# A hybrid decoder layer on one core: the order of the end of the kernel, of GpSimd's scatter and gather, and of the expert-row layout

## The reference

```python
h = h + moe_ffn(rms_norm(h, norm_ffn_w[l]), router_w[l], ...)   # top 4 of 32
#   per block of tokens of one expert e:
#     gu  = xb @ w_gate_up[e] + b_gate_up[e]
#     act = glu * sigmoid(1.702 * glu) * (lin + 1)      (clamped)
#     y   = (act @ w_down[e] + b_down[e]) * gate
#   out[token] += y
h = rms_norm(h, norm_final_w)
return h[:, N_META:]
```

## Time and profile before

| what | value |
|---|---|
| median of 3 runs | 1507.97 us (1507.8 to 1509.02) |
| the profiled execution, its time | 1512.59 us |
| its span, first to last instruction | 1511.0 us |
| TensorE busy | 1486.2 us (98%) |
| VectorE, ScalarE, GpSimd busy | 618.4, 255.5, 331.2 us |
| mean granted TensorE clock | 0.998 of full |
| bytes moved by DMA | 484.29 MB, 321 GB/s over the span |

### The profile page before, as it was taken

One profiled execution on the slowest core, in us unless ns is written; L12 is line 12 of the kernel. 1 busy time (PEld: TensorE's weight loads), 2 busy tenths in 40 slices (PEclk: granted clock), 3 DMA queues, 4 the chain that ended last, 5 costly groups with the idle time before them and its releaser, 6 DMA issues.

```text
span 1511.0 us, 38177 instructions
## 1 busy us (share of the span) xinstructions
PE 1486.2 (98%) x15435; PEld 793.7 (53%) x15435; DVE 618.4 (41%) x1268; ACT 255.5 (17%) x348; POOL 331.2 (22%) x518
## 2 busy tenths in 40 slices
PE   8999999999999999999999999999999999999997
PEld 6998998977873333443344333343333433334443
DVE  6667989868445312321132211222112321113226
ACT  3533433356231000000000000000000000000002
POOL 2000000000023432332223322233222233222330
PEclk9999999999999999999999999999999999999999
DMA  3642232322338999999999999999999999999976
GB/s 135 248 162 86 112 112 111 148 102 81 154 129 294 412 417 418 419 416 418 419 419 417 413 414 410 416 415 409 413 406 414 411 414 410 412 416 413 411 313 278
DMA packets 81367, 484.29 MB, mean 321 GB/s; under 512 B 17518, under 2 KB 18162, under 8 KB 26418
## 3 DMA queue, kind: packets, MB, share of 16 engines
q1 hardware_dynamic: 66066, 459.14, 74.9%
q0 software_dynamic: 15264, 24.63, 4.4%
HBM read 467.54 MB, written 25.00 MB: 326 GB/s over the span
## 4 chain that ended last, share of the span: by engine, by line
PE 69%; DMA 19%; SPq 6%; DVE 4%; issue 1%; ACT 1%; POOL 0%; DVEq 0%; ACTq 0%; POOLq 0%
PE bank L1816 42%; DMA ring<-in_moe 17%; PE bank L1497 15%; SPq L490 6%; PE bank L1688 6%; DVE w_lo L962 1%; DMA ring<-in_w_in 1%; PE bank L1625 1%; PE bank L1628 1%; PE bank L1757 0%; PE bank L1640 0%; PE bank L1626 0%; PE bank L1655 0%; DVE reg_tq L1052 0%; DMA reg_vcs<-in_xT 0%
## 5 line engine op out<-in xcount | busy, mean ns | idle before, releaser
L1816 PE MATMUL bank<-ring,moe_f 128*32 128x512 f32 (+1 forms) x12216 | 995.9, 486 | 6.7 <-DMA ring<-in_moe 3.6
L1816 PEld LDWEIGHTS bank<-ring,moe_f 128*32 128x32 f32 x12216 | 388.7, 110 | 612.8 <-issue 370.2
L1405 DVE STREAM_TRANSPOSE moe_f<-bank 128x768 f32<-128x768 f32 x32 | 31.5, 983 | 629.6 <-PE bank L1816 622.5
L621 POOL DMA_INDIRECT moe_f<-n_scratch,idx_next x96 | 100.1, 1043 | 450.2 <-DVE moe_f L1387 426.6
L1497 PE MATMUL bank<-n_hi,w_hi 128*128 128x258 f32 (+2 forms) x608 | 190.6, 313 | 2.9 <-DVE w_lo L962 2.9
L1497 PE MATMUL bank<-n_lo,w_hi 128*128 128x258 f32 (+2 forms) x608 | 186.3, 306 | 0.0
L1497 PE MATMUL bank<-n_hi,w_lo 128*128 128x258 f32 (+2 forms) x608 | 186.3, 306 | 0.0
L906 ACT ACTIVATE moe_f<-moe_f 128x768 f32<-128x768 f32 x32 | 27.0, 844 | 735.2 <-DVE moe_f L1409 735.2
L1497 PEld LDWEIGHTS bank<-n_hi,w_hi 128*128 128x128 f32 x608 | 114.4, 188 | 10.9 <-issue 3.2
L1497 PEld LDWEIGHTS bank<-n_lo,w_hi 128*128 128x128 f32 x608 | 114.5, 188 | 6.8 <-issue 1.7
L1497 PEld LDWEIGHTS bank<-n_hi,w_lo 128*128 128x128 f32 x608 | 114.5, 188 | 5.5
(11 more groups left out here) (293 smaller groups left out, 1058.4 us busy)
## 6 DMA issues: line engine op xcount, KB each, us to landing
ring<-in_moe SPq DMA_DIRECT2D x381, 1024.0 KB, 26.6
ring<-in_w_in SPq DMA_DIRECT2D x24, 1024.0 KB, 5.9
expert_rows<-reg_k POOLq DMA_DIRECT2D x8, 1024.0 KB, 6.3
ring<-in_w_out SPq DMA_DIRECT2D x8, 1024.0 KB, 5.4
ring<-expert_rows SPq DMA_DIRECT2D x8, 1024.0 KB, 12.1
ring<-acs_scratch SPq DMA_DIRECT2D x4, 1024.0 KB, 6.7
idx_raw<-slot_table POOLq DMA_DIRECT2D x140, 0.8 KB
reg_vcs<-in_xT SPq DMA_DIRECT2D x4, 528.0 KB, 6.8
```

The lines of the kernel that those rows point to most:

```text
L621: g.indirect_dma_start(out=xg[:, n, :], out_offset=None, in_=n2_parts, in_offset=bass.IndirectOffsetOnAxis(ap=idx_next[:, 2 * n:2 * n + 1] ...
L1405: v.transpose(glu.rearrange("p b (g r) -> p g b r", g=GRANULES), gate).then_inc(gate_raw, 1)
L1816: ins = mm(out[l * LANE:(l + 1) * LANE, g * width:(g + 1) * width], x[:, at, g * LANE:(g + 1) * LANE], w[:, l * width:(l + 1) * width], st ...
```

## The change

Six edits. VectorE's activations of the last block go to a buffer of their own, `act_last`, without the wait for `dn_used`, outside the loop. In GpSimd's loop the scatter (with its wait) stands ahead of the gather and the list. The rows of `expert_rows` are ordered token by token (row t * 4 + k) where they are written (the value table) and where they are read. In the end VectorE adds the rows of tile m+1 before it scales the mean of tile m, and PE's part after that. The last tile is scaled and stored in two halves. The zeros of `reg_k` are written behind the constants. Four semaphores that nothing used are gone.

```diff
+        act_last = view(moe_f, 8448, FF_BLOCKS, BLOCK)
 # SP
-                rows = yk_d.rearrange("(k t) d -> t k d", k=TOPK)[m * P:(m + 1) * P]
+                rows = yk_d.rearrange("(t k) d -> t k d", k=TOPK)[m * P:(m + 1) * P]
-            for m in range(TT):
+            for m in range(TT - 1):
                 sp.wait_ge(o_ready, m + 1)
                 sp.dma_start(out_d[m * P:(m + 1) * P, :], o_sb[m]).then_inc(out_out, 16)
+            for hf in range(2):
+                c = slice(hf * 512, (hf + 1) * 512)
+                sp.wait_ge(o_ready, TT + hf)
+                sp.dma_start(out_d[(TT - 1) * P:, c], o_sb[TT - 1][:, c]).then_inc(out_out, 16)
 # GpSimd, start
-            steps.done(g.memset(reg_k[:, :], 0.0))
...
-            g.iota(v3[:, :, :, 1], pattern=[[P * LANES, TT], [SEQ * LANES, TOPK]], ...)
+            g.iota(v3[:, :, :, 1], pattern=[[P * TOPK * LANES, TT], [LANES, TOPK]], ...)
...
             pool.dma_start(table_d..., pad_tile).then_inc(table_filled, 16)
+            steps.done(g.memset(reg_k[:, :], 0.0))
+            steps.settled()
 # GpSimd, loop
+                hold((y_ready, j + 2))
+                scatter()
                 hold((xT_ready, j + 3))
                 gather()
                 base = pool.value_load(...)
                 list_rows(base)
-
-                hold((y_ready, j + 2))
-                scatter()
                 hold((idx_in, ...), (x_in, ...), (y_out, ...))
 # VectorE
-                dve.wait_ge(dn_used, j * DN + 2 * DN)
-                v.tensor_tensor(act_t, up, sig, ALU.mult).then_inc(act_ready, 1)
+                if not last:
+                    dve.wait_ge(dn_used, j * DN + 2 * DN)
+                v.tensor_tensor(act_last if last else act_t, up, sig, ALU.mult).then_inc(act_ready, 1)
...
-            with dve.Fori(2, n_blocks) as j:
+            with dve.Fori(2, ahead) as j:
                 activations(j, expert_of(j))
+            activations(ahead, last, last=True)
...
+            rows(0)
+            total(0)
             for m in range(TT):
+                if m + 1 < TT:
+                    rows(m + 1)
                 dve.wait_ge(h2_ss, TT + m + 1)
                 v.tensor_scalar(small[:, m:m + 1], ...).then_inc(o_ms, 1)
                 if m + 1 < TT:
-                    combine(m + 1)
+                    total(m + 1)
-                (root, reciprocal, scale of the whole tile)
+                scale(m)       # for the last tile in two halves of 512 columns
 # TensorE
-            down(n_blocks - 1, GU)
+            down(n_blocks - 1, GU, act_last)
```

More of the change, by code:

```diff
@@ L318, in build @@
         staged, conv_ready, xbc_ready = sem("staged"), sem("conv_ready"), sem("xbc_ready")
-        dt_done, dt_raw, dt_e = sem("dt_done"), sem("dt_raw"), sem("dt_e")
+        dt_done, dt_e = sem("dt_done"), sem("dt_e")
         acs_ready, wend_e, pk_ready, dtk_done, dtk_ready = (
@@ L339, in build @@
         first_kept, first_turned, stack_ready, xT_half = [sem("first_kept0"), sem("first_kept1")], sem("first_turned"), sem("stack_ready"), sem("xT_half")
-        n2T_done, n2T_ready, logit_done, top_ready, gate_e, m_ready = (
-            sem("n2T_done"), sem("n2T_ready"), sem("logit_done"), sem("top_ready"), sem("gate_e"), sem("m_ready"))
+        n2T_done, n2T_ready, logit_done, top_ready, gate_e = (
+            sem("n2T_done"), sem("n2T_ready"), sem("logit_done"), sem("top_ready"), sem("gate_e"))
         rank_done, pos_ready, table_out, list_ready, list_out, list_in = (
@@ L345, in build @@
             sem("idx_in"), sem("idx_moved"), sem("x_in"), sem("xT_ready"), sem("lane_ready"))
-        bias_in, up_raw, bias_ready = sem("bias_in"), sem("up_raw"), sem("bias_ready")
+        bias_in, bias_ready = sem("bias_in"), sem("bias_ready")
         gu_used, dn_used, gu_free, glu_ready, sig_ready, act_ready = (
@@ L524, in _ @@
             for m in range(TT):
-                rows = yk_d.rearrange("(k t) d -> t k d", k=TOPK)[m * P:(m + 1) * P]
+                rows = yk_d.rearrange("(t k) d -> t k d", k=TOPK)[m * P:(m + 1) * P]
                 for hf in range(2):
                     sp.dma_start(yk(m, hf), rows[:, 2 * hf:2 * hf + 2, :]).then_inc(yk_in[hf][m], 16)
-            for m in range(TT):
+            for m in range(TT - 1):
                 sp.wait_ge(o_ready, m + 1)
                 sp.dma_start(out_d[m * P:(m + 1) * P, :], o_sb[m]).then_inc(out_out, 16)
-            sp.wait_ge(out_out, 16 * TT)
+            for hf in range(2):
+                c = slice(hf * 512, (hf + 1) * 512)
+                sp.wait_ge(o_ready, TT + hf)
+                sp.dma_start(out_d[(TT - 1) * P:, c], o_sb[TT - 1][:, c]).then_inc(out_out, 16)
+            sp.wait_ge(out_out, 16 * (TT + 1))
         @block.gpsimd
@@ L562, in _ @@
             g.iota(v3[:, :, :, 0], pattern=[[P * LANES, TT], [0, TOPK]], base=0, channel_multiplier=LANES).then_inc(consts, 1)
-            g.iota(v3[:, :, :, 1], pattern=[[P * LANES, TT], [SEQ * LANES, TOPK]], base=0, channel_multiplier=LANES).then_inc(consts, 1)
+            g.iota(v3[:, :, :, 1], pattern=[[P * TOPK * LANES, TT], [LANES, TOPK]], base=0, channel_multiplier=TOPK * LANES).then_inc(consts, 1)
             b2 = blocks[:, 0:2 * EXPERTS].rearrange("p (e t) -> p e t", t=2)
@@ L1395, in _, with activations @@
             dve.wait_ge(bias_ready, 1)
-            def activations(j, e, follows=True, at=0):
+            def activations(j, e, follows=True, at=0, last=False):
                 def bias_col(k, b):
@@ L1436, in _ @@
             activations(1, 1, at=5)
-            with dve.Fori(2, n_blocks) as j:
+            ahead = dve.value_load(blocks[0:1, 2 * LIST + 5:2 * LIST + 6], min_val=EXPERTS - 1, max_val=LIST - 2)
+            with dve.Fori(2, ahead) as j:
                 activations(j, expert_of(j))
+            activations(ahead, last, last=True)
             roots[0] += 1
@@ L1460, in _, with rows @@
             ins.then_inc(diag_ready, 1)
-            def combine(m):
+            def rows(m):
                 dve.wait_ge(yk_in[1][m], 16)
@@ L1469, in combine, with total @@
                     acc = o_sb[m]
+            def total(m):
                 dve.wait_ge(part_done, m + 1)
@@ L1473, in combine, with scale @@
                                 ).then_inc(o_sum, 1)
-            combine(0)
+            def scale(m):
+                rooted()
+                steps.done(v.reciprocal(small[:, m:m + 1], small[:, m:m + 1]))
+                steps.settled()
+                for c in ([slice(0, D)] if m < TT - 1 else [slice(0, 512), slice(512, D)]):
+                    v.scalar_tensor_tensor(o_sb[m][:, c], o_sb[m][:, c], small[:, m:m + 1], w_fin[:, c], ALU.mult, ALU.mult
+                                           ).then_inc(o_ready, 1)
+            rows(0)
+            total(0)
             for m in range(TT):
+                if m + 1 < TT:
+                    rows(m + 1)
                 dve.wait_ge(h2_ss, TT + m + 1)
@@ L1479, in _ @@
                 if m + 1 < TT:
-                    combine(m + 1)
[L1481 to L1485, removed]
+                    total(m + 1)
+                scale(m)
         @block.tensor
@@ L1836, in gate_up, with down @@
                         between()
-            def down(j, moved=0):
+            def down(j, moved=0, x=act_t):
                 pe.wait_ge(act_ready, j + 2)
@@ L1849, in down @@
                         b = 2 * (q - GU) + u
-                        ins = lanes(3, QUARTER, act_t, b, slot(s)[:, u * D:(u + 1) * D], b == 0, b == FF_BLOCKS - 1)
+                        ins = lanes(3, QUARTER, x, b, slot(s)[:, u * D:(u + 1) * D], b == 0, b == FF_BLOCKS - 1)
                     ins.then_inc(dn_used, 1)
```

## The result

| | before | changed |
|---|---|---|
| median, first comparison (4 runs each) | 1508.49 us | 1518.23 us |
| ratio | | 1.0055, 95% interval 1.0044 to 1.0067 |
| profiled execution, span | 1511.0 us | 1519.2 us |
| mean granted TensorE clock | 0.998 | 0.994 |

The changed kernel is slower, by 8.3 us on the ratio; its interval runs from 6.6 to 10.1 us, and the two medians lie 9.7 us apart.

The account below looks back on a forecast made before the run. TensorE's work or DMA loads were taken to bound the blocks, then a chain of scatter, rows read back and TensorE's products; 6.1 + 0.2 - 0.4 = +5.9 us on 1507.97 gave 1513.9 us, range 1509.0 to 1517.0.

Parts of the forecast that it names:

- Release: At the end, TensorE's first product with the rows waits for last_of behind the last list: +6.1 us, ends 5.1 to 7.4.
- the cover: Steady blocks: the later gather still lands 9 us before VectorE wants the tokens, so it costs 0.
- The clock: First eight products after TensorE's longer idleness at the end run at a lower clock: +0.2 us, ends 0 and 2.2.
- Own buffer: TensorE's last down: the wait for VectorE's multiplication goes, TensorE gains 0.3 us there, worth 0 in the total.
- Rows first: VectorE's end: rows of tile 1 fill a 1.22 us wait, but TensorE's part bounds the sum: at most 0.1 us, taken as 0.
- Halves: Last tile's multiplication and store in two: -0.4 us net, ends +0.1 and -1.2.
- Zeros: Program's start: constants ready 1.8 us sooner, but a product then waits longer for ScalarE's squares: 0.
- Layout: Rows read back in one 8 KB run per partition: worth 0, as the loads have 6 us more to arrive.
- The fast landing: Rival at the end: the last list lands 2.6 us after issue, total +2.7 us, 1510.7; chance 0.08.
- No new wait: Rival at the end: the release of last_of never decides, only the halves count, 1507.5 us; chance 0.06.
- the weight loads gain: Rival in the 19 slow blocks: half of their 17.3 us to the DMA engines comes back, 1505.3 us; chance 0.09.
- my sign of being wrong: Product still waiting for expert_rows, list landing within 4 us, or the blocks' pace moving by more than 0.1 us.

Follow-up runs that it names:

- e1: Kernel before with only the order in GpSimd's loop changed, scatter ahead of gather and list: 1517.01 us against 1509.7, ratio 1.0047.
- e3: Changed kernel with GpSimd's last iteration cut to scatter, its landing and one move of indices, without last gather and list: 1507.19 us, 0.9982 of the kernel before.
- e5: Kernel before with the own buffer for the last activations alone: 1508.98 us against 1509.88, ratio 0.9995.
- e7: Kernel before with rows of tile m+1 ahead of the mean of tile m and the last tile in halves, alone: 1508.71 us against 1509.88, ratio 0.999.
- e12: Kernel before with scatter ahead of gather and list and the last iteration cut, no other edits: 1508.87 us against 1509.94, ratio 0.9991.
- e9: Kernel before with the zeros of reg_k behind the constants, alone, on another chip: 1533.14 us against 1532.83, ratio 1.0001.
- e6: Kernel before with expert_rows ordered token by token, alone: 1508.94 us against 1509.88, ratio 0.9992.
- e10: e3 plus two unused 128x512 products behind TensorE's last down, on the chip of e9: 1522.6 us, 0.9931 of the kernel before.
- e11: The changed kernel once more, on the chip of e9: 1530.58 us, 0.9988 of the kernel before.
- e4: Changed kernel with nine unused 128x512 products behind TensorE's last down: 1514.12 us, 1.0034 of the kernel before.

## Why the prediction was right

**The place and the sign** were right, on the chips of the first two groups and of the first comparison: list at the tail, `last_of` as the new release, the delay passed on in full, steady blocks unchanged. Measured and forecast side by side, from the profiles: list issued 9.37 us behind the eviction (forecast 9.4), landing 8.48 us (7.9, ends 6.85 and 8.43), first move to VectorE's copy 1.31 (1.30), copy to TensorE's start 1.37 (1.37). Release +6.63 us (+6.1), shown by e1 and, with the list left out, by e3. Two side readings were off without touching the sum. VectorE's idle time before the copy was 20.21 us, not some 16: the own buffer had let its last multiplication run earlier (e1, without that buffer, has 15.84). And the gather in a steady block starts 5.7 us behind the eviction where it had started 5.2 us ahead of it, so 10.9 us later and not "some 7"; the cover held all the same, as the pace shows.

**The clock** was mis-sized: I took +0.2 with an end of +2.2, it was +1.31. The sentence behind the 0.2, "the rows' clock was low for about 3.4 of those 4 us already", reads its window rightly. What failed is the conclusion that little was left to lose, which takes the clock to come back as soon behind the long gap as before. The kernel before in windows of 1 us:

```profile
1481.00:1482.00 1.00, 1.00 (x3) 0.29 (x2) 0.12 (x1) 1.00 (x1) 0.00 (x0) 0.63 0.98 406
...
1484.00:1485.00 1.00, 1.00 (x2) 0.28 (x2) 0.96 (x2) 0.00 (x0) 0.00 (x0) 0.66 1.01 414
1485.00:1486.00 1.00, 1.00 (x4) 0.48 (x3) 0.77 (x1) 0.00 (x0) 0.00 (x0) 1.00 1.05 426
```

There the clock was low from 0.6 to 4.0 us behind the start of the eight products. In the changed kernel it was low from their start to 6.1 us behind it. That is 2.7 us more at half the clock, worth 1.3; 0.6 of them come from the clock having fallen beforehand, 2.1 from its coming back later. The nearer row was the program's start, 0.95 us each; behind the gap it was 0.83. That the clock fell at all in the profiled kernel before looks like chance: e5, e7 and e12, with edits that hardly touch this place, kept it up. Against such an execution the clock's part is 3.0 us.

With 0.2 the forecast was +5.9. With the release, the clock and the store as measured it is 6.6 + 1.3 - 0.5 = +7.4, or +9.1 against an execution without the low clock; the ratio's 8.3 lies between them. Put on the stated 1507.97, the ratio gives 1516.3, inside the range of 1509.0 to 1517.0. The median of the first comparison, 1518.23, lies above it, 4.3 us over the stated 1513.9; 0.5 us of that is the higher median of the kernel before. So the range held narrowly, and its upper part was needed for a clock that I had priced at almost nothing.

**The small edits.** Own buffer: 0 on the path as forecast (e5), though it gives 0.05 us and not 0.3 on TensorE. Rows first: 0.07 us on one step and 0 at the end (e7), forecast at most 0.1. Halves: -0.5 (-0.4). Zeros: 0 (e9). Layout: 0 within its interval (e6); behind the late release it was forecast not to count, which no run tests by itself.

**The rivals.** The fast landing (by a store's 2.6 us) did not come: GpSimd was idle 6.42 us behind the issue of the list, whose DMAs took 5.7 us from issue to landing. The Trainium skill ("DMA: Bandwidth & Descriptors", the section on the anatomy of a GpSimd DMA) puts such a DMA at 2.0 us plus its bytes; this trace disagrees, and the measurement decides. "No new wait" is refuted by the row of L1905. The rival "the weight loads gain", given 0.09 and put on the DMA engines, has no part on the chips of the first two groups. On the third chip the blocks did get faster, by 0.4 us each, and with that the changed kernel was not slower. The rows there put the gain on a shorter stall of TensorE, which I had not thought of, and not on the weight loads; I had no rival for it, and my sign of being wrong, a pace that moves by more than 0.1 us, did come there.

## What to carry to other kernels

When work is moved behind a wait inside a loop, read the last iteration by itself: what was done in the shadow of something else there may now be the last thing that the code behind the loop waits for, even if its result is of no use. Cut the last iteration to what is still read: with the new order kept, such versions beat both kernels on one chip of either kind (e3, 0.9982; e10, 0.9931 with two filling products), and with no other edit the order then costs nothing (e12, 0.9991). Before pricing a wait of TensorE, look at how much of a low clock the products behind it already carry, and both where it starts and where it ends.

## What the runs showed that I had not expected

- The kernel before sat where a chance of a few tenths of a microsecond decides 1.7 us. Behind 2.24 and 2.07 us of idleness the eight products took 5.37 us; behind 1.97, 1.86, 1.71, 1.67 and 1.66 us they took 3.67. Behind 8.39, 8.93 and, on the third chip, only 4.73 us they took 6.35, 6.68 and 6.67.
- Chips differ beyond the interval of a comparison: the kernel before takes 1508 to 1510 us in three of the comparisons' groups and 1532.8 on the chip of e9 to e11, and the same change is 1.0055 in the first comparison and 0.9988 on that chip.
- Reading 8 KB in one run in place of two of 4 KB cuts SP's time to issue eight loads of 1 MB from 7.05 to 4.01 us, and brings TensorE's first product with them only 0.24 us nearer.
- GpSimd waits 5.9 to 7.2 us behind the issue of four DMAs of 0.8 KB while the DMA engines are full (e1 5.92, the changed kernel 6.42, e11 7.08, e4 7.21).
